# Weight panels of the memory's keys and values: ten loaded into rooms of their own, low parts split on VectorE; half of the output product moved into the last attention unit's steps

## The reference, cut to what matters

```
u = rms_norm(x, g_mix) @ w_in                     # 8 units of q, k, v: 4 of one attention, 4 of the other
ya = diff_attention(...)                          # channels 0 to 511 of y: units 0 to 3
yb = stick_breaking_attention(...)                # channels 512 to 1023: units 4 to 7
h  = x + concat(ya, yb) @ w_out                   # "wo", the output product
k, v = rms_norm(mem, g_mem) @ w_xkv               # 256 tokens of memory: "xk", "xv"
q  = rms_norm(h, g_cross) @ w_xq                  # "xq"
h  = h + softmax(q k^T / 16) v @ w_xo             # then the MLP, the final norm and the second block
```

## Time and profile before

| | us |
|---|---|
| median of three runs | 2530.85 |
| the profiled execution | 2540.15 |
| its span | 2538.3 |
| TensorE busy in the span | 2396.3 |
| last unit's steps (span 632.13 to 693.32) | 61.19 |
| output product up to the first panel of xk (to 792.41) | 99.09 |
| xk, the norm's sum, xv (to 863.54) | 71.13 |

### The profile page before, as it was taken

How to read it: one execution, slowest core, us unless ns; L and a number is a source line. 1 busy time by engine, 2 the same in 40 slices (tenths; PEclk the granted TensorE clock), 3 DMA queues, 4 the chain that set the end, 5 groups by cost and what they waited for, 6 DMA issues and landing times.

```text
span 2538.3 us, 35212 instructions
## 1 busy us (share of the span) xinstructions
PE 2396.3 (94%) x14684; PEld 1814.6 (71%) x14684; DVE 1114.8 (44%) x1471; ACT 855.0 (34%) x1475; POOL 586.2 (23%) x262
## 2 busy tenths in 40 slices
PE   6999989999898899899999999999999999999997
PEld 4777665555377776577888888888867677778885
DVE  5767654343651622453212112112242847476554
ACT  4333435555722321223203113113342622254321
POOL 2312111110134521231222212212223123223222
PEclk9999999999999999999999999999999999999999
DMA  3111101000312200011111111111221001100022
GB/s 141 58 42 50 34 26 50 34 30 25 121 42 83 91 25 25 25 49 36 50 50 45 47 42 58 42 50 50 91 77 50 26 26 34 44 26 12 3 101 75
DMA packets 36508, 126.06 MB, mean 50 GB/s; under 512 B 3856, under 2 KB 4368, under 8 KB 35984
## 3 DMA queue, kind: packets, MB, share of 16 engines
q1 hardware_dynamic: 30096, 103.30, 12.7%
q10 hardware_dynamic: 6272, 20.72, 2.2%
HBM read 114.57 MB, written 8.91 MB: 49 GB/s over the span
## 4 chain that ended last, share of the span: by engine, by line
PE 86%; DVE 8%; ACT 4%; issue 1%; POOL 1%; ACTq 0%; DVEq 0%; POOLq 0%
PE PS L179 21%; PE PS L181 21%; PE PS L180 21%; PE PS L1764 2%; PE PS L805 2%; PE PS L790 2%; PE PS L645 1%; PE PS L668 1%; PE PS L1002 1%; DVE y_r L189 1%; PE PS L817 1%; POOL w_lo L189 1%; PE PS L830 1%; PE PS L979 1%; PE PS L647 1%
## 5 line engine op out<-in xcount | busy, mean ns | idle before, releaser
L189 POOL TENSOR_TENSOR w_lo<-w_raw,w_hi 128x1024 fp32r<-128x1024 f32 x160 | 402.8, 2517 | 638.1 <-ACT w_hi L185 631.9
L179 PE MATMUL PS<-u_r,w_hi 128*128 128x512 f32 x1280 | 520.4, 407 | 18.4 <-DVE y_r L189 5.2
L181 PE MATMUL PS<-u_r,w_lo 128*128 128x512 f32 x1280 | 507.7, 397 | 0.0
L180 PE MATMUL PS<-arena_r,w_hi 128*128 128x512 f32 (+1 forms) x1152 | 441.0, 383 | 0.0
L226 POOL TENSOR_TENSOR w_hi<-w_raw,const 128x1024 fp32r<-128x1024 f32 x78 | 154.8, 1985 | 1198.3 <-PE PS L179 1036.3
L179 PEld LDWEIGHTS PS<-u_r,w_hi 128*128 128x128 f32 x1280 | 242.0, 189 | 91.8 <-issue 9.9
L181 PEld LDWEIGHTS PS<-u_r,w_lo 128*128 128x128 f32 x1280 | 242.0, 189 | 57.3
L180 PEld LDWEIGHTS PS<-arena_r,w_hi 128*128 128x128 f32 x1152 | 218.4, 190 | 44.4 <-issue 0.7
L179 PE MATMUL PS<-h_r,w_hi 128*128 128x512 f32 x512 | 210.6, 411 | 4.1 <-DVE u_r L381 3.9
L179 PE MATMUL PS<-y_r,w_hi 128*128 128x512 f32 x512 | 203.9, 398 | 0.0
L181 PE MATMUL PS<-h_r,w_lo 128*128 128x512 f32 x512 | 203.0, 396 | 0.0
(11 more groups left out here) (388 smaller groups left out, 3601.0 us busy)
## 6 DMA issues: line engine op xcount, KB each, us to landing
w_raw<-in_w SPq DMA_DIRECT2D x184, 512.0 KB, 3.5
h<-in_xT ACTq DMA_DIRECT2D x1, 4096.0 KB, 13.7
u<-parked_stream ACTq DMA_DIRECT2D x1, 4096.0 KB, 12.8
out<-arena SPq DMA_DIRECT2D x16, 256.0 KB, 2.0
parked_stream<-h ACTq DMA_DIRECT2D x6, 512.0 KB, 2.6
h<-in_xT SPq DMA_DIRECT2D x8, 256.0 KB, 7.4
h<-in_xT ACTq DMA_DIRECT2D x8, 256.0 KB, 9.2
const<-in_const ACTq DMA_DIRECT2D x1, 1408.0 KB, 14.0
```

Of the source, the lines that this page charges most:

```text
L179: first = pe.matmul(out, a[0], b[0], start=start, stop=False)
L180: pe.matmul(out, a[0], b[1], start=False, stop=False)
L181: return first, pe.matmul(out, a[1], b[0], start=False, stop=stop)
L189: return e.tensor_tensor(out, x, hi_part.bitcast(F), ALU.subtract)
```

## The change

What each part does:

1. In the last unit, the first halves (input chunks 0 to 3, the channels of units 0 to 3) of wo's output panels 2 to 7 are computed in the twelve steps, one piece ("w", p, h) of 12 matmuls in each. Their weights come as three packed panels, each holding chunks 0 to 3 of two output panels; the second halves (chunks 4 to 7) come as three more. Panels 0 and 1 stay whole. VectorE adds the twelve first halves into `hT` in the same steps.
2. y's chunks are split as they become ready, one at a time at steps 8 to 11 of unit 6 (chunks 0 to 3) and at steps 3, 5, 7 and 10 of unit 7 (`Y1_AT`); a last half of chunk 7 after the last step. Pieces of chunks 0 to 6 are 1024 columns wide.
3. The ada sums of unit 7 move to steps 9 and 11 of unit 6 and step 1 of unit 7; the chunk ("ada", 6) to step 8; ("ada", 7) to step 4, copied out by VectorE. The 4 MB transfer of x is issued three steps earlier.
4. TensorE's last step with v comes behind the first piece of wo.
5. Of the sixteen panels of the keys and values, ten land outside `w_raw`: 2 and 3 (and again 6 and 7) in `Vc`, 10 to 15 in `qcT`. All sixteen, and the first of xq, get their high part on ScalarE (`kv_high`) and their low part on VectorE (`kv_low`).
6. The norm's sum (x) comes behind panel 1 and not between panels 7 and 8. Its two roots come at panels 2 and 5, and the 16 pieces of norm and split of h are spread over panels 3 to 15 (`X_BESIDE`): one beside each, two beside 11, 12 and 13.

The core of the diff (the later panels' counters shift by five, which changes no work):

```diff
@@ sb_chunks
             if w == UNITS:
-                return [("ada", u, 0)] if s == 7 else []
+                return ([("ada", u, 0)] if s == 4 else []) + [("w",) + WO_HALVES[s]]
...
+            if u == UNITS - 2 and s in (8, 11):
+                return [("ada", u, 0)] if s == 8 else []
...
+        WO_HALVES = [(p, h) for p in range(2, KC) for h in range(2)]
+        Y1 = [(k, 0, T) for k in range(KC - 1)] + [(KC - 1, h * HALF, (h + 1) * HALF) for h in range(2)]
+        Y1_AT = {(2, 8): 0, (2, 9): 1, (2, 10): 2, (2, 11): 3, (3, 3): 4, (3, 5): 5, (3, 7): 6, (3, 10): 7}
...
+        def late_chunk_dve(dve, c):
+            n, (what, p, h) = CHUNK[c], c
+            if n == CHUNK["w", 2, 0]:
+                dve.wait_ge(*chunk_done(("t", UNITS - 1, 1)))
+                dve.wait_ge(S("x_in"), 80)
+                dve.wait_ge(S("x_late"), 128)
+            dve.wait_ge(S("proj_mm"), n + 1)
...
+            dve.tensor_tensor(dst, dst, bank(n % 2), ALU.add).then_inc(S("proj_evac"), 1)
@@ chunk_pe
+            elif what == "w":
+                a, x = divmod(w - 2, 2)
+                if x == 0 and h == 0:
+                    panel_in(pe, UNIT_MAIN + a)
+                m = chunk_product(pe, UNIT_MAIN + a, b, u_y1, h, ready=y1_ready(pe, h) if w == 2 and h == 0 else None, order=range(4),
+                                  free=x == 0 and h == 0, at=4 * x)
@@ sb_dve
-                at = (2, 3, 5) if j == 0 else (1, 3, 5)
-                if s in at:
-                    ada_dve(dve, N_DA + j, at.index(s))
+                at = {(j, s): (N_DA + j, x) for j in range(3) for x, s in enumerate((2, 3, 5) if j == 0 else (1, 3, 5))}
+                at.update({(2, 9): (UNITS - 1, 0), (2, 11): (UNITS - 1, 1), (3, 1): (UNITS - 1, 2)})
+                if (j, s) in at:
+                    ada_dve(dve, *at[j, s])
+                if (j, s) in Y1_AT:
+                    y1_dve(dve, Y1_AT[j, s])
+                if j == 3:
+                    for c in sb_chunks(j, s):
+                        if c[0] != "t":
+                            late_chunk_dve(dve, c)
@@ keys and values
+        def kv_high(act, n):
+            act.wait_ge(S("weight_free"), KV_AT + n + CREDIT)
+            raw, sem, v = kv_raw(n)
+            act.wait_ge(sem, v)
+            high(act, w_hi[:, n % 2, :], raw).then_inc(S("w_high"), 1)
+        def kv_low(dve, n):
+            dve.wait_ge(S("w_high"), KV_AT + n + 1)
+            low(dve, w_lo[:, n % 2, :], kv_raw(n)[0], w_hi[:, n % 2, :]).then_inc(S("w_split"), 1)
...
+        X_BESIDE = {3: 1, 4: 1, 5: 1, 6: 1, 7: 1, 8: 1, 9: 1, 10: 1, 11: 2, 12: 2, 13: 2, 14: 1, 15: 1}
@@ VectorE
             for q in range(8, 16):
                 add_wo(q)
+                if q == 13:
+                    kv_low(dve, 0)
...
+            kv_low(dve, 1)
+            for n in range(16):
+                if n < 15:
+                    kv_low(dve, n + 2)
+                for h, k in x_beside(n):
+                    split_dve(dve, "x", h, in_(yT), in_u, in_y, (in_(hT), lambda k: vcol("g_cross", k), x_rs, "x"),
+                              ks=[k] if k < KC - 1 else [k, KC])
@@ ScalarE (the high parts of panels 0 and 1 at pieces 12 and 15 of wo)
+            for n in range(16):
+                j = n % 8
+                act.wait_ge(S("gemm_mm"), GEMM_FROM["xk"] + n + 1)
+                act.activation((KcT if n < 8 else VcT)[:, j, :], bank(j % 4)[:, :MEM], ACT.Copy)\
...
+                if n < 15:
+                    kv_high(act, n + 2)
+                if n in (2, 5):
+                    norm_root(act, "x", n // 5, x_rs)
...
+                for h, k in x_beside(n):
+                    x_split(h, [k])
@@ TensorE
-            for g in range(SB_ALL + 2):
+            for g in range(SB_ALL + 1):
                 sb_pe(pe, g)
             for q in range(16):
-                piece_pe(pe, "wo", UNIT_MAIN, NATURAL, q, pair(in_u, in_y), ready=wait_split(pe, "y1", q) if q < 2 else None)
+                wo_pe(pe, q)
+                if q == 0:
+                    sb_pe(pe, SB_ALL + 1)
...
+            for n in range(16):
+                kv_pe(pe, n)
+                if n == 1:
+                    for h in range(2):
+                        norm_pe(pe, "x", h)
```

More of the change, by code:

```diff
@@ L386, in in_, with chunk_product @@
             return lambda k, lo, hi: t[:, k, lo:hi]
-        def chunk_product(pe, g, b, x, h, width=T, ready=None, order=range(KC), free=None, inner=None):
+        def chunk_product(pe, g, b, x, h, width=T, ready=None, order=range(KC), free=None, inner=None, at=0):
             w = min(width, HALF)
@@ new lines, in wo_pe @@
+        def wo_pe(pe, q):
+            p, h = NATURAL[q]
+            a, x = divmod(p - 2, 2)
+            g = UNIT_MAIN + (3 + p if p < 2 else 5 + a)
+            first = h == 0 and (p < 2 or x == 0)
+            if first:
+                panel_in(pe, g)
+            pe.wait_ge(S("wo_evac"), q + 1)
+            chunk_product(pe, g, bank(q % 4), u_y1, h, ready=y1_ready(pe, h) if q < 2 else None, order=range(0 if p < 2 else 4, KC),
+                          free=first, at=0 if p < 2 else 4 * x - 4).then_inc(S("gemm_mm"), 1)
@@ L563, in chunk_act @@
             n, (what, w, h) = CHUNK[c], c
+            if what == "w" or c == ("ada", UNITS - 1, 0):
+                return
             act.wait_ge(S("proj_mm"), n + 1)
@@ L928, in dyn, with kv_raw, kv_pe, x_beside @@
             return t[:, bass.ds(k, n), lo:hi]
+        KV_AT = UNIT_MAIN + 8
+        def kv_raw(n):
+            if n >= 10 and n < 16:
+                return qcT[:, n - 8, :], S("v_raw" + str((n - 10) // 2)), 32
+            if n < 8 and n % 4 >= 2:
+                return Vc[:, n % 2, :], S("k_raw" + str(n % 2)), 16 * (n // 4 + 1)
+            return w_raw[:, n % 2, :], w_in[n % 2], 16 * (UNIT_MAIN + 4 + [0, 1, 4, 5, 8, 9, 16].index(n) // 2) + 16
+        def kv_high(act, n):
[6 more added lines that the diff above has]
+            low(dve, w_lo[:, n % 2, :], kv_raw(n)[0], w_hi[:, n % 2, :]).then_inc(S("w_split"), 1)
+        def kv_pe(pe, n):
+            panel_in(pe, KV_AT + n)
+            pe.wait_ge(S("xk_evac" if n < 8 else "xv_evac"), n % 8 + 1)
+            chunk_product(pe, KV_AT + n, bank(n % 4), mem_split, 0, MEM, ready=wait_split(pe, "mem", 0) if n == 0 else None)\
+                .then_inc(S("gemm_mm"), 1)
+        X_BESIDE = {3: 1, 4: 1, 5: 1, 6: 1, 7: 1, 8: 1, 9: 1, 10: 1, 11: 2, 12: 2, 13: 2, 14: 1, 15: 1}
+        def x_beside(n):
+            done = sum(X_BESIDE.get(x, 0) for x in range(n))
+            return [divmod(i, KC) for i in range(done, done + X_BESIDE.get(n, 0))]
         XQ_BANKS = (6, 7)
@@ L2399, in _ @@
             dve.wait_ge(S("sb_acc"), SB_ALL)
[L2400 to L2404, removed]
+            dve.sem_inc(S("wo_evac"), 2)
+            y1_dve(dve, KC)
             for k in range(1, KC):
@@ L2620, in _ @@
                 sb_act(act, g)
-            act.wait_ge(S("sb_acc"), SB_ALL)
+            y1_act(act, KC)
             act.dma_start(mraw, memT_d).then_inc(S("mem_in"), 16)
-            for h in range(2):
-                split_act(act, "y1", h, in_(yT), in_u, lambda k: [(S("da_y_ready"), k + 1) if k < N_DA else (S("sb_acc"), SB_N * (k - N_DA + 1))])
             act.wait_ge(S("mem_in"), 16)
```

125 lines of the change are left out of this document (79 added, 46 removed).

## The result

The changed kernel takes 2522.15 us (median of ten runs, 2515.85 to 2525.58) against 2536.73 us for the kernel before (ten runs, 2529.42 to 2541.38). The ratio is 0.9942, 95% interval 0.9928 to 0.9955: 14.6 us faster (11.4 to 18.3). The forecast was 2509 us, range 2499 to 2521, 21.5 us faster. The sign held, the time fell 1 us outside the range. What the title calls half of the output product is three eighths of it: twelve pieces of 12 matmuls, 144 of 384. The profiled execution took 2524.78 us, span 2523.0.

A forecast was written before the change was run, and what follows sets the result against it. TensorE, 86% of the chain, was taken as the bound, so time is won where it waits or runs at its lower clock. Gains 12.9 + 8.6 = 21.5 took 2540.15 to 2518.6, on the median's scale 2509 us; range 2499 to 2521.

The forecast's parts named there:

- the one to the median: Whole kernel: profiled execution lay 9.3 over the median, so the forecast 2518.6 became 2509.3 us on the median's scale.
- A(1): Last unit: wo pieces in the steps remove TensorE's 8.66 us idle less a residue of 1.0; gain 7.66.
- A(2): Last unit: denser steps win back 1.65 us of the 1.8 lost at TensorE's lower clock.
- A(3): Start of wo: waits of 5.2 us for y's low parts go, with the lower clock behind them, about 2.5; gain 7.7.
- A(4): Costs: 1.7 us delay over unit 6's steps 8 to 11, 2.2 wait for the first wo piece's fourth chunk.
- A: Last unit and wo, 160.28 us before: the part's terms sum to a gain of 12.9, bounds 3 and 17.
- B: Keys and values, 71.13 us before: rounds of 3.82 and 5.08, stage 62.5 with the clock; gain 8.6.
- R1: Keys and values: rounds stay at 4.1 us, so B gives 0; 2517.9 us, chance 0.13.
- R2: Last unit: ScalarE or VectorE keeps TensorE waiting 8 to 9 us, A gives 3; 2519 us, chance 0.13.
- R3: Keys and values: ScalarE's queue hides the norm's wait under TensorE, B nearer 52, gain 19; 2499 us, chance 0.09.
- R4: Panels 0 to 15: shorter waits still bring 1.2 GHz, B loses 17; together 12 slower, 2543 us, chance 0.04.

The follow-up runs named there:

- unit_order: Changed kernel with VectorE's work in the last two units reordered: add of the wo piece, then y's low part, then ada sum; ratio 0.9895 to the kernel before.
- kv_late: Changed kernel with high and low part of each piece of h one round after its norm; ratio 0.9872 to the kernel before.
- kv_only: Kernel before with only the keys' and values' part of the change, last unit and wo as before; ratio 0.9981 to the kernel before.
- add_first: Changed kernel with VectorE's add of the wo piece ahead of ada sum and y's low part in the last unit; ratio 0.9912 to the kernel before.
- late_two_rooms: Changed kernel with h's high and low parts one round later and all key and value panels through w_raw's two rooms; ratio 0.9879 to the kernel before.

## Why the prediction was wrong

**Two steps failed: the one to the median, and the clock's term in the gain.** "It lay 9.3 over the median" took the median of three runs, 2530.85, as the kernel's time. Ten runs gave 2536.73, 29 in the second comparison 2534.43. That is 5.9 of the 13.2 us missed, and the range held the bounds of the costs and nothing for the base, with runs of one kernel 12 us apart. Another 6.9 are the gain, 14.6 measured for 21.5, and the rest is rounding. Either miss alone would have stayed in the range: 2536.73 with the forecast gain gives 2515.2, and 2530.85 with the measured gain 2516.3. The first of these would have been in the range by luck, with a gain half as large again as the measured one.

**The gain.** 21.5 forecast; 18.1 in the profiles' stages; 14.6 (11.4 to 18.3) in the comparison, 16.5 (10.9 to 21.8) in the next. 3.4 are in terms of the sum, the other 3.5 within the interval.
- A(1), filler: right. Waits for the Exp 1.0, as the residue. The sign named for it, no such wait over 0.3, was too strict: one was 0.8. The unit took 90.89 and not about 87.
- A(2), clock: wrong, and the largest miss. It had "1.65 back", since the steps are denser; the last unit held two spells of 3.4 and not one, 0.96 granted and not 0.97, so 1.7 were lost in place of 1.65 won, 3.4 of the miss. The filler brought two waits of its own, and the spells stood behind these. In unit_order, with these waits gone, the clock is 1.00.
- A(3), start of wo: right. No wait for y, full clock; wo with its share in the steps fell by 99.09 - 33.4 - 58.52 = 7.2, forecast 7.7 less 0.2.
- A(4): the wait for the fourth chunk 1.96, forecast 2.2. Unit 6's last steps lost 0.4, not 1.7: ScalarE had more room there than I gave it. Not seen: the add of the filler of step 3 stands behind y's low part on VectorE, and the chunk two further waits for that bank, 1.20.
- A in all: 10.5 for 12.9. The terms as measured, 7.7 - 1.7 + 7.2 - 2.0 - 1.2 - 0.4, give 9.6; the 0.9 left is not assigned.
- B: rounds 3.81 (3.82 forecast) and 5.07 (5.08), stage 61.88 (61.5 without the clock). Within it, panel 8 waited 2.42 for a semaphore behind ScalarE's seventh round, which I had not counted; the next round was 2.92 for it, so 0.8 was lost. The lower clock behind the waits of 2 came in this profile not among the panels but in xq, and cost 1.6, forecast 1.0. B in all: 7.6 for 8.6.
- A's lower bound, 3, isn't the sum of its terms' bounds: 5.2 less 10 is below nothing. The range was drawn from the rivals, so this didn't decide.
- GpSimd's hold on VectorE under the steps cost nothing visible: VectorE is busy 47.10 of 90.89, and the low parts that the two new waits stand behind took 1.22 and 1.23, unheld.

R1 and R2 are out (rounds of 3.81; TensorE's waits in the last unit 4.2 and not 8 to 9, A 10.5 and not 3). R3 described not this kernel but kv_late, 50.43 for its 52. R4 is out: the panels' clock was 1.00. Where a spell did come among them, behind panel 8's wait in kv_only, unit_order and add_first, it cost 0.5 to 0.7, not 17.

## What to carry to other kernels

When work is moved between two engines, follow the handovers once round: a part that waits for the other engine's part that waits for the first sets the round, here 3.81 where TensorE needed 2.95, and taking the consumer one round later removed it without moving any work. On an in-order engine, put what the bottleneck waits for ahead of what nobody waits for; that took 3.2 us of waits out here, and with the lower clock behind them up to 6.5. Give the range something for the base: a median of three runs lay 5.9 below that of ten and 3.6 below that of 29.

## What was not expected of the hardware

A wait that stood ahead of a spell at 1.2 GHz in one profile did not in another: behind the 1.96 ahead of the first filler the spell came in the changed kernel, behind the 1.95 at the same place in late_two_rooms it did not. Where a spell falls decides its price. With rounds of 5.07, it came at the start of xq in five profiles of seven (xq 27.6, 1.6 lost); in kv_only and add_first it came one panel earlier, where TensorE had 2 us to spare in the round, and cost nothing (xq 26.0). In add_first:

```profile
837.52 0.39 PE L179 MATMUL PS<-arena_r,w_hi 128*128 128x256 f32 x1 [1.95 <-DVE w_lo L189]
...
842.59 0.50 PE L179 MATMUL PS<-u_r,w_hi 128*128 128x512 f32 x1 [0.44 <-DVE w_lo L189]
```

The panel of 837.52 ran slowly and used up the wait: 0.44 are left in front of xq of the changed kernel's 1.97. What comes behind xq, untouched by any of these edits, varied from 1639.8 to 1651.4 us between profiles.
